# Merge stage: both norms applied where products leave PSUM, unscaled split tiles feed the next product, and the per-layer input split in a buffer of its own

## The chip, the cores and the metric

The kernel runs on one core of one Trainium2 chip. The metric is the device time of one execution in microseconds (us), from the first instruction to the end. Kernels are compared by the median of several executions on the same chip. The profile shows one such execution, instruction by instruction.

## The reference

Two transformer-like blocks run over 512 tokens of 1024 features, in fp32. The change lies in the last part of the second block:

```python
        merged = gates[..., 0, :] * (attn @ w_up_attn[i]) + gates[..., 1, :] * (rw @ w_up_rwkv[i])
        x = x + merged @ w_out[i]
        hf = rms_norm(x, norm_ffn[i])
        x = x + jnp.square(jax.nn.relu(hf @ w_ff1[i])) @ w_ff2[i]
        hp = rms_norm(x, norm_ple[i])
        x = x + (p[i] @ w_ple[i]) * jax.nn.sigmoid(hp @ w_ple_gate[i])
```

`rms_norm(x, g)` is `x * rsqrt(mean(x * x) + 1e-6) * g`, with the mean over the 1024 features of a token and the gain `g` per feature. The hidden width of the feed-forward part is 4096, and `p` has 256 features per token. The root is one number per token, and a product over features is linear, so it can be multiplied in before or behind a product; relu lets a positive factor through as well.

## The kernel before

Everything is held with features on the 128 partitions and the 512 tokens along the free dimension, so 1024 features are `KT` = 8 row tiles of 128 x 512. The merge stage (`merge_block`) takes the last quarter of the kernel's time.

**Products in three passes.** Each fp32 operand is split into a high part in TensorE's fp32r type and the low rest. One product step is three matmuls (`three_pass`): weights high by data high, weights low by data high, weights high by data low. A tile of output, 128 features by 512 tokens, takes 8 rows of 3 matmuls, so 24. The matmuls stand in lines 240 to 242, whichever phase they serve.

**The weight ring.** Weights come in slots of 128 x 2048, which hold two output tiles' columns. A ring of two raw buffers is filled by SyncE's queue. ScalarE copies a slot to `w_hi` (line 215), VectorE subtracts to get `w_lo` (line 228), each one slot ahead of TensorE and each only after TensorE has finished the slot that used the buffer before. `hi_next` and `lo_next` are these two steps; they stand first in every slot's body on their engines.

**The phases**, in order: `up` (4 slots, 16 short tiles), `out` (4 slots), then four times `ff1[g]` and `ff2[g]` (4 slots each), `ple` (1 slot, 8 tiles of two rows), `pgate` (4 slots). Output tiles go round four PSUM banks. TensorE waits for the tile four before it to have left PSUM (`tile_free`), and at a phase's first tile for all of the phase before it. At a phase's first tile it also waits, row by row, for the data (`ready`).

**Who takes the tiles out.** In `out` and `ff2`, VectorE adds the tile to `x` (line 2798). In `ff1`, ScalarE does Relu out of PSUM (2750) and Square (2752) into the high part, VectorE squares again and subtracts for the low part (2832, 2835). In `ple`, VectorE copies (2848). In `pgate`, ScalarE does Sigmoid out of PSUM (2770), VectorE multiplies by the `ple` tile and adds to `x` (2858, 2860), and SyncE stores.

**The norms.** During `out` and the last `ff2`, ScalarE squares each finished tile of `x` (2699), and GpSimd adds the squares up (`add_squares`). Behind the last tile, TensorE multiplies the sum by a matrix of ones (2673), ScalarE takes the root of 128 x 512 (2714), VectorE its reciprocal (2779), and for each of 8 rows VectorE multiplies `x` by gain and reciprocal (2785), ScalarE copies the high part (2719) and VectorE subtracts the low part (2788). Only then is a row ready for the next product. `p` is split on ScalarE (2759) and VectorE (2842) behind the last `ff2`, into `y_hi` and `y_lo`, ahead of `ple`.

The helpers `sum_tokens` (line 318), `spread_tokens` (327) and `on_diagonal` (333) exist already and serve the earlier stages. `sum_tokens` multiplies the squares, as the stationary operand, by a column of ones, 128 tokens at a time: the sum comes out with one token per partition, 128 x 4. `on_diagonal` puts these 512 numbers on the diagonals of four 128 x 128 matrices. `spread_tokens` multiplies ones by these matrices, and so copies the numbers into a row on all partitions, 128 x 512.

Of the kernel before, what the change touches and what calls it, by code (L numbers as in the profile page):

```python
# [21 lines left out]
P = 128  # L22
D = 1024
# [238 lines left out]
def gemm_slot(pe, nc, R, ph, j, q, r, u_hi, u_lo, outs, rows=range(KT), cols=SLOT, ready=None):  # L262
# [5 lines left out]
    for m in range(ph.tiles):  # L268
# [2319 lines left out]
def merge_block(nc, io, C, PV, h, attn_t, rw_t, gate_pre):  # L2588

    with ExitStack() as ctx:  # L2590
# [15 lines left out]
        for _ in range(GROUPS):  # L2606
# [19 lines left out]
        squared, summed, std_done, rs_done, normed, u_hi_done, u_done = (  # L2626
            sem(n) for n in ("squared", "summed", "std_done", "rs_done", "normed", "u_hi_done", "u_done"))
# [3 lines left out]
        relu_hi, relu_sq, relu_done, p_loaded, p_hi, p_done, ple_read, ple_gated, x_done, stored = (  # L2631
            sem(n) for n in ("relu_hi", "relu_sq", "relu_done", "p_loaded", "p_hi", "p_done", "ple_read", "ple_gated", "x_done", "stored"))
# [28 lines left out]
        @block.gpsimd  # L2661
        def _(pool):
            for n in range(2):
                if n:
                    pool.wait_ge(summed, n)
                add_squares(pool, nc, sq, sq_sum, squared, sq_added, n, KT)

        @block.tensor
        def _(pe):
            def norm(n):  # L2670

                pe.wait_ge(sq_added, KT * n)
# [9 lines left out]
            norm(1)  # L2682
            for g in range(GROUPS):
                products(ff1[g], u_hi, u_lo, ready=(u_done, 0) if g == 0 else None)
                products(ff2[g], y_hi, y_lo, ready=(relu_done, KT * g))
            pe.wait_ge(p_done, 1)
            products(ple, y_hi, y_lo, range(2), D)
            norm(2)
            products(pgate, u_hi, u_lo, ready=(u_done, KT))

        @block.scalar
        def _(act):
            def squares(n, ph):

                def tile(t):
                    act.wait_ge(R.tile_free, ph.c0 + t + 1)
                    if t >= 2:
                        act.wait_ge(sq_added, KT * (n - 1) + t - 1)
# [77 lines left out]
        def _(dve):  # L2776
            def norm(n):
                dve.wait_ge(std_done, n)
                nc.vector.reciprocal(rs, std).then_inc(rs_done, 1)  # L2779
                dve.wait_ge(rs_done, n)  # L2780
                for k in range(KT + 1):
                    if k < KT:
                        if k >= 4:
                            dve.wait_ge(u_done, KT * (n - 1) + k - 3)
# [202 lines left out]
```

## Time and profile before

| | |
|---|---|
| median of 3 runs | 2008.22 us (2004.9 to 2009.2) |
| the profiled execution's own time | 2009.05 us |
| its span, first to last instruction | 2007.2 us |
| TensorE matmul busy | 1792.2 us, 89% |
| TensorE weight load busy | 1533.6 us, 76% |
| VectorE busy | 1017.4 us, 51% |
| ScalarE busy | 670.2 us, 33% |
| GpSimd busy | 88.5 us, 4% |
| mean granted TensorE clock | 0.945 of full speed |

Times in the profile count from the start of the span. PE is TensorE, DVE VectorE, ACT ScalarE, POOL GpSimd, SPq SyncE's DMA queue. A matmul's bar is longer than its share of the pace, since matmuls overlap; the pace is read from one start to the next. The arrow at the end of a row names what ended the idle time before it.

### The profile page before, as it was taken

What the parts mean: (1) busy time and instruction counts of PE and PEld (TensorE: products, weight loads), DVE (VectorE), ACT (ScalarE), POOL (GpSimd) and SP (SyncE); (2) the same over time, 40 slices, a digit from 0 to 9 for tenths busy, and PEclk for the clock granted to TensorE, in tenths of its full rate; (3) what the DMA queues carried; (4) which work ended last, traced back from release to release, by engine and by line L of the source; (5) the groups of instructions that cost most, each with busy time, mean ns of one, the idle gap of its engine ahead of it and who ended that gap; (6) DMA issues with size and microseconds to landing.
All of it is one profiled execution on the core that took longest, in us unless ns stands there. A gap on an engine that the chain in (4) does not pass through costs nothing. (4 is left out here: it accounts for less than half of the span.)

```text
span 2007.2 us, 38445 instructions
## 1 busy us (share of the span) xinstructions
PE 1792.2 (89%) x17084; PEld 1533.6 (76%) x17084; DVE 1017.4 (51%) x1505; ACT 670.2 (33%) x1091; POOL 88.5 (4%) x115
## 2 busy tenths in 40 slices
PE   5999789888999999988999948888679899999978
PEld 5898767888989989787677737767568688788867
DVE  4146564455644645456554346765655534343444
ACT  3242233433433423343332233333143323232322
POOL 6000000010000000100000000000002000000020
PEclk9999888988999999989999969999889899999999
DMA  5211130111222232312122100000052222222211
GB/s 156 85 64 43 54 105 1 59 49 52 96 101 89 84 105 85 105 59 84 64 79 93 39 23 4 4 4 10 2 220 85 71 97 95 94 98 91 102 66 63
DMA packets 29260, 144.57 MB, mean 72 GB/s; under 512 B 6315, under 2 KB 9659, under 8 KB 14508
## 3 DMA queue, kind: packets, MB, share of 16 engines
q1 hardware_dynamic: 25116, 134.10, 18.7%
q0 software_dynamic: 3696, 7.35, 1.2%
q8 instruction: 132, 2.16, 0.4%
q10 hardware_dynamic: 288, 0.73, 0.1%
q14 instruction: 28, 0.23, 0.0%
HBM read 134.82 MB, written 8.91 MB: 72 GB/s over the span
## 5 line engine op out<-in xcount | busy, mean ns | idle before, releaser
L228 DVE TENSOR_TENSOR w_w_lo<-w_w_raw,w_w_hi 128x2048 fp32r<-128x2048 f32 x67 | 153.5, 2291 | 182.3 <-ACT w_w_hi L215 181.9
L240 PE MATMUL f_bank<-u_hi,w_w_hi 128*128 128x258 f32 x704 | 203.3, 289 | 12.3 <-DVE w_w_lo L228 6.1
L241 PE MATMUL f_bank<-u_hi,w_w_lo 128*128 128x258 f32 x704 | 202.2, 287 | 0.0
L242 PE MATMUL f_bank<-u_lo,w_w_hi 128*128 128x258 f32 x704 | 200.7, 285 | 0.0
L240 PE MATMUL g_bank<-g_u_hi,g_w_hi 128*128 128x512 f32 x384 | 152.8, 398 | 17.1 <-DVE g_u_lo L2788 13.6
L241 PE MATMUL g_bank<-g_u_hi,g_w_lo 128*128 128x512 f32 x384 | 151.1, 394 | 0.0
L242 PE MATMUL g_bank<-g_u_lo,g_w_hi 128*128 128x512 f32 x384 | 151.1, 394 | 0.0
L240 PE MATMUL g_bank<-g_y_hi,g_w_hi 128*128 128x512 f32 x336 | 132.9, 396 | 18.5 <-DVE g_w_lo L228 11.7
L240 PEld LDWEIGHTS f_bank<-u_hi,w_w_hi 128*128 128x128 f32 x704 | 135.1, 192 | 13.7 <-issue 6.4
L215 ACT ACTIVATE g_w_hi<-g_w_raw 128x2048 fp32r<-128x2048 f32 x45 | 85.9, 1909 | 174.2 <-PE g_bank L242 171.8
L215 ACT ACTIVATE w_w_hi<-w_w_raw 128x2048 fp32r<-128x2048 f32 x67 | 127.6, 1904 | 32.0 <-PE f_bank L242 32.0
L242 PEld LDWEIGHTS f_bank<-u_lo,w_w_hi 128*128 128x128 f32 x704 | 136.0, 193 | 0.0
L241 PEld LDWEIGHTS f_bank<-u_hi,w_w_lo 128*128 128x128 f32 x704 | 135.3, 192 | 0.0
L242 PE MATMUL g_bank<-g_y_lo,g_w_hi 128*128 128x512 f32 x336 | 132.5, 394 | 0.0
L241 PE MATMUL g_bank<-g_y_hi,g_w_lo 128*128 128x512 f32 x336 | 132.3, 394 | 0.0
L228 DVE TENSOR_TENSOR g_w_lo<-g_w_raw,g_w_hi 128x2048 fp32r<-128x2048 f32 x45 | 103.2, 2292 | 48.3 <-ACT g_w_hi L215 48.1
L240 PEld LDWEIGHTS g_bank<-g_u_hi,g_w_hi 128*128 128x128 f32 x384 | 73.0, 190 | 40.0 <-issue 20.1
L1641 PE MATMUL a_bank<-u_hi,w_w_hi 128*128 128x512 f32 x240 | 99.4, 414 | 4.2 <-DVE a_shift L1878 3.6
L1643 PE MATMUL a_bank<-u_hi,w_w_lo 128*128 128x512 f32 x240 | 99.0, 412 | 0.0
L1645 PE MATMUL a_bank<-u_lo,w_w_hi 128*128 128x512 f32 x240 | 98.9, 412 | 0.0
L240 PEld LDWEIGHTS g_bank<-g_y_hi,g_w_hi 128*128 128x128 f32 x336 | 64.1, 191 | 34.5 <-issue 17.0
L2798 DVE TENSOR_TENSOR h<-g_bank,h 128x512 f32<-128x512 f32 x40 | 27.7, 692 | 115.0 <-PE g_bank L242 115.0
(460 smaller groups left out, 4047.5 us busy)
## 6 DMA issues: line engine op xcount, KB each, us to landing
g_w_raw<-in_w_ff SPq DMA_DIRECT2D x32, 1024.0 KB, 4.8
w_w_raw<-in_w_in SPq DMA_DIRECT2D x30, 1024.0 KB, 4.8
w_w_raw<-in_w_ffn_in SPq DMA_DIRECT2D x22, 1024.0 KB, 4.8
w_w_raw<-in_w_ffn_out SPq DMA_DIRECT2D x12, 1024.0 KB, 4.8
w_w_raw<-in_w_o SPq DMA_DIRECT2D x4, 1024.0 KB, 4.9
gate_pre<-rw_t POOLq DMA_DIRECT2D x16, 256.0 KB, 2.3
g_w_raw<-in_w_up SPq DMA_DIRECT2D x4, 1024.0 KB, 9.5
g_branch<-gate_pre SPq DMA_DIRECT2D x4, 1024.0 KB, 12.5
```

The source lines that it names most:

```text
L215: nc.scalar.activation(R.hi[:, r, 0:size], R.raw[:, r, 0:size], ACT.Copy).then_inc(R.hi_done, 1)
L228: nc.vector.tensor_tensor(R.lo[:, r, 0:size], R.raw[:, r, 0:size], R.hi[:, r, 0:size].bitcast(F32), ALU.subtract).then_inc(R.split, 1)
L240: nc.tensor.matmul(out, w_hi, u_hi, start=start, stop=False)
L241: nc.tensor.matmul(out, w_lo, u_hi, start=False, stop=False)
L242: return nc.tensor.matmul(out, w_hi, u_lo, start=False, stop=stop)
L1641: nc.tensor.matmul(tile_bank(g), w_hi, u_hi[:, k, :], start=k == 0, stop=False)
L1643: nc.tensor.matmul(tile_bank(g), w_lo, u_hi[:, k, :], start=False, stop=False)
L1645: last = nc.tensor.matmul(tile_bank(g), w_hi, u_lo[:, k, :], start=False, stop=k == KT - 1)
L2798: nc.vector.tensor_tensor(x[:, t, :], bank[:, (2 * r + m) % 4, :], x[:, t, :], ALU.add).then_inc(R.tile_free, 1)
```

## The change

Both norms are applied later. While `x` is finished tile by tile, ScalarE copies `x` times the gain to `y_hi` and VectorE makes `y_lo` from the same product, without the factor per token. `ff1` and `pgate` read these; the relu results go to `u_hi` and `u_lo` in exchange. The factor per token is applied to the tiles as they leave PSUM, both in `ff1` and in `pgate`, and both times on VectorE. In `ff1` VectorE takes over Relu with it, as one operation; in `pgate` VectorE multiplies, and ScalarE's Sigmoid then reads the result from SBUF.

The factor itself is computed with the small products: `sums` on TensorE behind the first tile of `ff1[0]` (or behind the fourth tile of `ple`), root and reciprocal on 128 x 4, `spread` behind the next tile of `ff1[0]` (or behind the first tile of `pgate`), and a copy from PSUM on ScalarE, for which VectorE waits. GpSimd adds seven squares instead of eight; the eighth is summed by TensorE directly. `p` is split right behind `up` into buffers of its own.

```diff
 def gemm_slot(...):
         last.then_inc(R.tile_done, 1)
+        if then:
+            then(m)
...
-        sq, std, rs = branch[:, 8:10, :], branch[:, 10, :], branch[:, 11, :]
+        p_hi, p_lo = sb("p_hi", [P, 2, GRID], F32R), sb("p_lo", [P, 2, GRID], F32R)
+        sq = branch[:, 8:10, :]
+        rows = sb("rows", [P, 3, GRID])
+        sq_sum, rs, diag = rows[:, 0, :], rows[:, 1, :], rows[:, 2, :].rearrange("p (a b) -> p a b", a=NB)
...
         @block.gpsimd
-                    pool.wait_ge(summed, n)
-                add_squares(pool, nc, sq, sq_sum, squared, sq_added, n, KT)
+                    pool.wait_ge(tok_sum, n)
+                add_squares(pool, nc, sq, sq_sum, squared, sq_added, n)
...
         @block.tensor
-            def norm(n):
-                pe.wait_ge(sq_added, KT * n)
-                nc.tensor.matmul(bank[:, 4, :], C("ones"), sq_sum, start=True, stop=True).then_inc(summed, 1)
+            def sums(n):
+                pe.wait_ge(sq_added, (KT - 1) * n)
+                sum_tokens(pe, nc, C, bank[:, 4, :], sq_sum, P, NB, True, False)
+                pe.wait_ge(squared, KT * n)
+                sum_tokens(pe, nc, C, bank[:, 4, :], sq[:, (KT - 1) % 2, :], P, NB, False, True).then_inc(tok_sum, 1)
+            def spread(n):
+                pe.wait_ge(tok_diag, n)
+                spread_tokens(pe, nc, C, [bank[:, 5, :]], diag, P, NB).then_inc(row_done, 1)
+            def after_first(j, m):
+                if j == 0:
+                    (sums, spread)[m](1)
+            def after_ple(j, m):
+                if m == 3:
+                    sums(2)
+            def after_gate(j, m):
+                if j == 0 and m == 0:
+                    spread(2)
-            norm(1)
             for g in range(GROUPS):
-                products(ff1[g], u_hi, u_lo, ready=(u_done, 0) if g == 0 else None)
-                products(ff2[g], y_hi, y_lo, ready=(relu_done, KT * g))
+                products(ff1[g], y_hi, y_lo, ready=(u_done, 0) if g == 0 else None, then=after_first if g == 0 else None)
+                products(ff2[g], u_hi, u_lo, ready=(relu_done, KT * g))
-            products(ple, y_hi, y_lo, range(2), D)
-            norm(2)
-            products(pgate, u_hi, u_lo, ready=(u_done, KT))
+            products(ple, p_hi, p_lo, range(2), D, then=after_ple)
+            products(pgate, y_hi, y_lo, ready=(u_done, KT), then=after_gate)
...
         @block.scalar
                     act.wait_ge(R.tile_free, ph.c0 + t + 1)
+                    nc.scalar.activation(y_hi[:, t, :], x[:, t, :], ACT.Copy, scale=gain(NORMS[n], t)).then_inc(u_hi_done, 1)
...
             def norm(n):
-                act.wait_ge(summed, n)
-                nc.scalar.activation(std, bank[:, 4, :], ACT.Sqrt, scale=1.0 / D, bias=EPS).then_inc(std_done, 1)
-            def norm_hi(n):
-                for k in range(KT):
-                    act.wait_ge(normed, KT * (n - 1) + k + 1)
-                    nc.scalar.activation(u_hi[:, k, :], tmp[:, k % 4, :], ACT.Copy).then_inc(u_hi_done, 1)
+                act.wait_ge(tok_sum, n)
+                nc.scalar.activation(stat, bank[:, 4, 0:NB], ACT.Sqrt, scale=1.0 / D, bias=EPS).then_inc(tok_std, 1)
+                act.wait_ge(row_done, n)
+                nc.scalar.activation(rs, bank[:, 5, :], ACT.Copy).then_inc(row_read, 1)
...
             each_slot(act, up, up_slot)
+            act.wait_ge(p_loaded, 16)
+            nc.scalar.activation(p_hi[:], p_raw[:], ACT.Copy).then_inc(p_hi_done, 1)
             squares(1, out)
-            norm(1)
-            norm_hi(1)
...
                 def relu_slot(j, q, r, g=g):
                     hi_next(act, nc, R, ff1[g], j, q, r)
+                    if g == 0 and j == 0:
+                        norm(1)
                     for m in range(2):
                         t = 2 * j + m
-                        act.wait_ge(R.tile_done, ff1[g].c0 + t + 1)
-                        if KT * g + t >= 4:
-                            act.wait_ge(relu_done, KT * g + t - 3)
-                        nc.scalar.activation(branch[:, 4 + t % 4, :], bank[:, (2 * r + m) % 4, :], ACT.Relu).then_inc(R.tile_free, 1)
                         act.wait_ge(R.tile_free, ff1[g].c0 + t + 1)
-                        nc.scalar.activation(y_hi[:, t, :], branch[:, 4 + t % 4, :], ACT.Square).then_inc(relu_hi, 1)
+                        nc.scalar.activation(u_hi[:, t, :], branch[:, 4 + t % 4, :], ACT.Square).then_inc(relu_hi, 1)
...
             weights(ple)
             norm(2)
-            norm_hi(2)
             def pgate_slot(j, q, r):
                 hi_next(act, nc, R, pgate, j, q, r)
...
-                    act.wait_ge(R.tile_done, pgate.c0 + t + 1)
-                    nc.scalar.activation(branch[:, 8 + t, :], bank[:, (2 * r + m) % 4, :], ACT.Sigmoid).then_inc(R.tile_free, 1)
+                    act.wait_ge(R.tile_free, pgate.c0 + t + 1)
+                    nc.scalar.activation(branch[:, 8 + t, :], branch[:, 8 + t, :], ACT.Sigmoid).then_inc(gated, 1)
...
         @block.vector
             def norm(n):
...
+                dve.wait_ge(tok_std, n)
+                nc.vector.reciprocal(stat, stat).then_inc(tok_rs, 1)
+                dve.wait_ge(tok_rs, n)
+                on_diagonal(dve, nc, C, diag, stat, P, NB).then_inc(tok_diag, 1)
+            def add_to_x(ph, n=None):
+                def low(t):
+                    dve.wait_ge(u_hi_done, KT * (n - 1) + t + 1)
+                    nc.vector.scalar_tensor_tensor(y_lo[:, t, :], x[:, t, :], gain(NORMS[n], t), y_hi[:, t, :].bitcast(F32),
+                                                   ALU.mult, ALU.subtract).then_inc(u_done, 1)
...
                         nc.vector.tensor_tensor(x[:, t, :], bank[:, (2 * r + m) % 4, :], x[:, t, :], ALU.add).then_inc(R.tile_free, 1)
+                        if n and t:
+                            low(t - 1)
                 each_slot(dve, ph, slot)
+                if n:
+                    low(KT - 1)
...
             each_slot(dve, up, up_slot)
-            add_to_x(out)
-            norm(1)
+            dve.wait_ge(p_hi_done, 1)
+            nc.vector.tensor_tensor(p_lo[:], p_raw[:], p_hi[:].bitcast(F32), ALU.subtract).then_inc(p_done, 1)
+            add_to_x(out, 1)
...
                     lo_next(dve, nc, R, ff1[g], j, q, r)
+                    if g == 0 and j == 0:
+                        norm(1)
+                        dve.wait_ge(row_read, 1)
                     for m in range(2):
...
+                        dve.wait_ge(R.tile_done, ff1[g].c0 + t + 1)
+                        if KT * g + t >= 4:
+                            dve.wait_ge(relu_hi, KT * g + t - 3)
+                        nc.vector.scalar_tensor_tensor(a, bank[:, (2 * r + m) % 4, :], 0.0, rs, ALU.max, ALU.mult).then_inc(R.tile_free, 1)
...
-                add_to_x(ff2[g])
-            dve.wait_ge(p_hi, 1)
-            nc.vector.tensor_tensor(y_lo[:, 0:2, :], p_raw[:], y_hi[:, 0:2, :].bitcast(F32), ALU.subtract).then_inc(p_done, 1)
+                add_to_x(ff2[g], 2 if g == GROUPS - 1 else None)
...
             norm(2)
+            dve.wait_ge(row_read, 2)
             def pgate_slot(j, q, r):
                 lo_next(dve, nc, R, pgate, j, q, r)
...
-                    dve.wait_ge(R.tile_free, pgate.c0 + t + 1)
+                    dve.wait_ge(R.tile_done, pgate.c0 + t + 1)
+                    nc.vector.tensor_tensor(branch[:, 8 + t, :], bank[:, (2 * r + m) % 4, :], rs, ALU.mult).then_inc(R.tile_free, 1)
+                    dve.wait_ge(gated, t + 1)
```

## Rows read from the trace of the kernel before

**Rows 1.** Groups by line and shape, 1440 to 2007 us: busy, mean ns, idle before.

```profile
L228 DVE TENSOR_TENSOR g_w_lo<-g_w_raw,g_w_hi 128x2048 fp32r<-128x2048 f32 x45 | 103.2, 2292 | 48.3 <-ACT g_w_hi L215 48.1
L215 ACT ACTIVATE g_w_hi<-g_w_raw 128x2048 fp32r<-128x2048 f32 x45 | 85.9, 1909 | 174.2 <-PE g_bank L242 171.8 <-DMA g_w_raw<-in_w_up 1.7 <-DVE g_u_lo L2788 0.8
...
L2798 DVE TENSOR_TENSOR h<-g_bank,h 128x512 f32<-128x512 f32 x40 | 27.7, 692 | 115.0 <-PE g_bank L242 115.0
...
L2752 ACT ACTIVATE g_y_hi<-g_branch 128x512 fp32r<-128x512 f32 x32 | 20.3, 633 | 1.0
...
L2785 DVE SCALAR_TENSOR_TENSOR g_branch<-h,params,g_branch 128x512 f32<-128x512 f32 x16 | 11.8, 747 | 0.1
```

**Rows 2.** Windows: PE, PEld, DVE, ACT, POOL busy (count); granted clock; DMA share; GB/s.

```profile
1562.00:1580.00 18.00, 9.56 (x22) 5.61 (x23) 13.41 (x17) 7.69 (x12) 1.26 (x1) 0.62 0.00 0
1709.00:1754.00 45.00, 43.80 (x192) 35.96 (x192) 16.09 (x14) 9.20 (x7) 0.00 (x0) 1.00 0.26 94
1936.00:1939.00 3.00, 3.00 (x9) 2.30 (x8) 2.65 (x2) 0.00 (x0) 0.00 (x0) 0.50 0.02 8
```

**Rows 3.** Timeline around the first norm: start, length, engine, line, instruction.

```profile
1561.02 0.69 DVE L2798 TENSOR_TENSOR h<-g_bank,h 128x512 f32<-128x512 f32 x1 [4.75 <-PE g_bank L242]
...
1579.60 0.50 PE L240 MATMUL g_bank<-g_u_hi,g_w_hi 128*128 128x512 f32 x1 [0.30 <-DVE g_u_lo L2788]
```

**Rows 4.** Timeline, last `ff2` tile to `pgate`.

```profile
1931.57 0.69 DVE L2798 TENSOR_TENSOR h<-g_bank,h 128x512 f32<-128x512 f32 x1 [4.75 <-PE g_bank L242]
...
1935.41 0.50 PE L240 MATMUL g_bank<-g_y_hi,g_w_hi 128*128 128x512 f32 x1 [3.87 <-DVE g_y_lo L2842]
...
1947.83 0.39 PE L242 MATMUL g_bank<-g_y_lo,g_w_hi 128*128 128x512 f32 x1
...
1948.26 0.69 DVE L2848 COPY g_branch<-g_bank 128x512 f32<-128x512 f32 x1 [0.67 <-PE g_bank L242]
...
1962.92 0.50 PE L240 MATMUL g_bank<-g_u_hi,g_w_hi 128*128 128x512 f32 x1 [0.30 <-DVE g_u_lo L2788]
```

**Rows 5.** Timeline, two ordinary changes of phase.

```profile
1619.49 0.60 ACT L2750 ACTIVATE g_branch<-g_bank 128x512 f32<-128x512 f32 x1 [4.18 <-PE g_bank L242]
...
1620.18 0.47 PE L240 MATMUL g_bank<-g_y_hi,g_w_hi 128*128 128x512 f32 x1 [0.73 <-issue]
...
1663.60 0.39 PE L242 MATMUL g_bank<-g_y_lo,g_w_hi 128*128 128x512 f32 x1
1664.02 0.69 DVE L2798 TENSOR_TENSOR h<-g_bank,h 128x512 f32<-128x512 f32 x1 [4.75 <-PE g_bank L242]
...
1664.86 0.47 PE L240 MATMUL g_bank<-g_u_hi,g_w_hi 128*128 128x512 f32 x1 [0.88 <-DVE h L2798]
```

**Rows 6.** Timeline, `up` to `out`.

```profile
1516.93 0.47 PE L240 MATMUL g_bank<-g_u_hi,g_w_hi 128*128 128x512 f32 x1 [0.83 <-issue]
...
1521.74 2.29 DVE L228 TENSOR_TENSOR g_w_lo<-g_w_raw,g_w_hi 128x2048 fp32r<-128x2048 f32 x1
```

**Rows 7.** Timeline, the same small products in the layer's attention stage.

```profile
850.68 0.39 PE L242 MATMUL f_bank<-f_y_lo,w_w_hi 128*128 128x512 f32 x1
851.12 1.05 PE L318 MATMUL a_bank<-consts,f_a 128*128 128x1 f32 x8
...
857.45 2.08 PE L327 MATMUL a_bank<-a_s,consts 128*128 128x128 f32 x8 [3.89 <-DVE a_s L333]
...
897.85 1.05 PE L327 MATMUL a_bank<-a_s,consts 128*128 128x128 f32 x8
898.66 0.36 PE L1604 MATMUL a_bank<-w_w_hi,u_hi 128*128 128x256 f32 x1
```

**Rows 8.** Groups by line and shape, whole kernel.

```profile
L1234 DVE SCALAR_TENSOR_TENSOR m_at<-m_bank,m_work 128x400 f32<-128x400 f32 x16 | 9.2, 575 | 28.6 <-PE m_bank L773 14.6 <-PE m_bank L777 14.0
```

**Rows 9.** Timeline, end of the kernel.

```profile
2002.78 0.60 ACT L2770 ACTIVATE g_branch<-g_bank 128x512 f32<-128x512 f32 x1 [4.84 <-PE g_bank L242]
...
2004.86 0.33 SPq L2658 DMA_DIRECT2D out<-h  x1
```

More of the change, by code:

```diff
@@ L259, in lo_ahead, with gemm_slot @@
     lo_slot(dve, nc, R, q + 1, r)
-def gemm_slot(pe, nc, R, ph, j, q, r, u_hi, u_lo, outs, rows=range(KT), cols=SLOT, ready=None):
+def gemm_slot(pe, nc, R, ph, j, q, r, u_hi, u_lo, outs, rows=range(KT), cols=SLOT, ready=None, then=None):
     pe.wait_ge(R.split, 2 * q + r + 1)
@@ L308, in add_squares @@
         if k:
-            pool.wait_ge(added, KT * n + k)
+            pool.wait_ge(added, count * n + k)
             nc.gpsimd.tensor_tensor(total, total, sq[:, k % 2, :], ALU.add).then_inc(added, 1)
@@ L2615, in merge_block @@
         p_raw = sb("p_raw", [P, 2, GRID])
-        sq, std, rs = branch[:, 8:10, :], branch[:, 10, :], branch[:, 11, :]
-        sq_sum_t = sb("sq_sum", [P, GRID])
-        sq_sum = sq_sum_t[:]
-        tmp = branch[:, 12:16, :]
+        p_hi, p_lo = sb("p_hi", [P, 2, GRID], F32R), sb("p_lo", [P, 2, GRID], F32R)
+        sq = branch[:, 8:10, :]
+        rows = sb("rows", [P, 3, GRID])
+        sq_sum, rs, diag = rows[:, 0, :], rows[:, 1, :], rows[:, 2, :].rearrange("p (a b) -> p a b", a=NB)
+        stat_t = sb("stat", [P, NB])
+        stat = stat_t[:]
         bank = ctx.enter_context(nc.psum_tensor("g_bank", [P, 8, 512], F32))
@@ L2625, in merge_block @@
         sq_added = sem("sq_added")
-        squared, summed, std_done, rs_done, normed, u_hi_done, u_done = (
-            sem(n) for n in ("squared", "summed", "std_done", "rs_done", "normed", "u_hi_done", "u_done"))
+        squared, tok_sum, tok_std, tok_rs, tok_diag, row_done, row_read, u_hi_done, u_done = (
+            sem(n) for n in ("squared", "tok_sum", "tok_std", "tok_rs", "tok_diag", "row_done", "row_read", "u_hi_done", "u_done"))
         split_hi, split_lo, gate_open, both, m_hi, m_done = (
@@ L2630, in merge_block @@
         gate_loaded = [sem(f"gate_loaded{k}") for k in range(4)]
-        relu_hi, relu_sq, relu_done, p_loaded, p_hi, p_done, ple_read, ple_gated, x_done, stored = (
-            sem(n) for n in ("relu_hi", "relu_sq", "relu_done", "p_loaded", "p_hi", "p_done", "ple_read", "ple_gated", "x_done", "stored"))
+        relu_hi, relu_sq, relu_done, p_loaded, p_hi_done, p_done, gated, ple_gated, x_done, stored = (
+            sem(n) for n in ("relu_hi", "relu_sq", "relu_done", "p_loaded", "p_hi_done", "p_done", "gated", "ple_gated", "x_done", "stored"))
         branches = (attn_t, rw_t)
@@ L2664, in _, with products @@
                 if n:
-                    pool.wait_ge(summed, n)
-                add_squares(pool, nc, sq, sq_sum, squared, sq_added, n, KT)
+                    pool.wait_ge(tok_sum, n)
+                add_squares(pool, nc, sq, sq_sum, squared, sq_added, n)
         @block.tensor
         def _(pe):
-            def norm(n):
-                pe.wait_ge(sq_added, KT * n)
-                nc.tensor.matmul(bank[:, 4, :], C("ones"), sq_sum, start=True, stop=True).then_inc(summed, 1)
-            def products(ph, hi, lo, rows=range(KT), cols=SLOT, ready=None):
-                each_slot(pe, ph, lambda j, q, r: gemm_slot(pe, nc, R, ph, j, q, r, hi, lo, outs, rows, cols, ready))
+            def sums(n):
[6 more added lines that the diff above has]
+                spread_tokens(pe, nc, C, [bank[:, 5, :]], diag, P, NB).then_inc(row_done, 1)
+            def products(ph, hi, lo, rows=range(KT), cols=SLOT, ready=None, then=None):
+                each_slot(pe, ph, lambda j, q, r: gemm_slot(pe, nc, R, ph, j, q, r, hi, lo, outs, rows, cols, ready,
+                                                            then and (lambda m: then(j, m))))
+            def after_first(j, m):
[7 more added lines that the diff above has]
+                    spread(2)
             pe.wait_ge(split_lo, 2)
@@ L2696, in tile @@
                     act.wait_ge(R.tile_free, ph.c0 + t + 1)
+                    nc.scalar.activation(y_hi[:, t, :], x[:, t, :], ACT.Copy, scale=gain(NORMS[n], t)).then_inc(u_hi_done, 1)
                     if t >= 2:
[L2698 removed]
+                        act.wait_ge(sq_added, (KT - 1) * (n - 1) + t - 1)
                     nc.scalar.activation(sq[:, t % 2, :], x[:, t, :], ACT.Square).then_inc(squared, 1)
@@ L2777, in norm @@
             def norm(n):
[L2778 to L2784, printed above, removed]
-                        nc.vector.scalar_tensor_tensor(tmp[:, k % 4, :], x[:, k, :], gain(NORMS[n], k), rs, ALU.mult, ALU.mult).then_inc(normed, 1)
-                    if k:
-                        dve.wait_ge(u_hi_done, KT * (n - 1) + k)
-                        nc.vector.tensor_tensor(u_lo[:, k - 1, :], tmp[:, (k - 1) % 4, :], u_hi[:, k - 1, :].bitcast(F32),
-                                                ALU.subtract).then_inc(u_done, 1)
-            def add_to_x(ph):
+                dve.wait_ge(tok_std, n)
[7 more added lines that the diff above has]
+                                                   ALU.mult, ALU.subtract).then_inc(u_done, 1)
                 def slot(j, q, r):
@@ L2834, in relu_slot @@
                         dve.wait_ge(relu_hi, KT * g + t + 1)
-                        nc.vector.tensor_tensor(y_lo[:, t, :], branch[:, 12 + t % 4, :], y_hi[:, t, :].bitcast(F32),
+                        nc.vector.tensor_tensor(u_lo[:, t, :], branch[:, 12 + t % 4, :], u_hi[:, t, :].bitcast(F32),
                                                 ALU.subtract).then_inc(relu_done, 1)
```

3 lines of the change are left out of this document (removed).

## Prediction

> **What bounds the kernel now.** I read the groups of instructions of the merge stage first. The two engines that feed the weight ring are idle far more than busy: ScalarE's ring copy waited 171.8 us for TensorE's last product, and VectorE's subtraction for the ring took 2.29 us per slot of about 11 us [rows 1]. So TensorE sets the pace, and only a place where TensorE is held up can be won. The windows show where. In an ordinary stretch of 45 us TensorE is busy 43.8 us at granted clock 1.00, that is 2.4 GHz; from 1562 to 1580 us it is busy about half and the clock is at 0.62, and between 1936 and 1939 us it works without a pause at 0.50, that is 1.2 GHz [rows 2]. The timeline names the three holes: the norm between `out` and `ff1[0]` [rows 3], the split of `p` ahead of `ple`, and the norm between `ple` and `pgate` [rows 4]. Everything else in the stage is eight ordinary changes of phase, each a wait for the last tile to leave PSUM [rows 5].
>
> The pitch of one matmul at full clock: the first of `ff2[0]` starts at 1620.18, the last of its 192 at 1663.60, so 0.227 us each [rows 5]. A tile of 24 takes 5.45 us, a slot 10.9 us.
>
> **First norm.** VectorE's addition of the last `out` tile starts at 1561.02. TensorE then reaches row 7 of the first `ff1` tile (its last three matmuls) at 1579.60, since rows 0 to 6 are done piecemeal behind the norm [rows 3]. That is 18.6 us, and 0.1 more for the slow restart, 18.7. After the change this transition is like that from `ff2` to `ff1`: addition at 1664.02, first matmul at 1664.86, 0.84 later [rows 5]; row 7 follows 21 pitches and 0.1 of restart later, at 5.7. `low(6)` and `low(7)` are ready 1.5 and 2.3 us after the addition starts (0.69, and 0.75 each [rows 1]), before rows 6 and 7 are reached. Gain 13.0 us.
>
> **Split of p.** It moves to the end of `up`. Before, the addition at 1931.57 was followed by the first `ple` matmul at 1935.41 [rows 4], 3.84 us; after, by 0.84. Gain 3.0. The `ple` matmuls ran from 1935.41 to the start of the last at 1947.83, 12.4 us for 47 pitches, where 0.227 each make 10.7 [rows 2, 4]. With the hole gone I take the clock to stay up: gain 1.7. In its new place the split stands in the first `out` slot, ahead of the ring's copy on ScalarE and of its subtraction on VectorE. It has half the elements of those, so it costs at most 1.91 and 2.29 us [rows 1]. The subtraction, at 1521.74 before, then begins by 1524.1 and ends by 1526.4; TensorE asks for that slot at 1516.93 plus 10.9, 1527.8 [rows 6]. Covered with 1.4 us to spare even so; price nothing. Without that cover it would cost its excess alone, once.
>
> **Second norm.** From the last copy of `ple` at 1948.26 to row 7 at 1962.92 [rows 4], 14.7 and 0.1; after, 5.7 again. Gain 9.1. The gains add to 26.8 us.
>
> **What is put on TensorE.** `sums` is two calls of four products of one column, which the trace shows as two instructions each, sixteen in all; `spread` is eight. Eight of the former take 1.05 us including 0.25 of the last one's length, so 0.11 a piece, and the change of kind in front costs 0.2 (850.68 to 851.12, where 0.23 is usual) [rows 7]. Sixteen: 1.8, with 0.3 for both ends 2.1. For `spread`, 897.85 to 898.66 is 0.8, with the ends 1.1. Twice 3.2 is 6.4 us, all on TensorE's path. From below I take 0.1 each for 48, or 4.8; from above the row at half clock, 2.08 us for eight [rows 7], which makes `spread` and `sums` twice as dear, 12.8.
>
> **Evictions.** Relu moves from ScalarE (0.60) to VectorE, with the row of reciprocals multiplied in. Nearest rows: 0.75 for this operation with 512 columns from SBUF [rows 1], and 0.575 with 400 columns from PSUM [rows 8], so 0.69 to 0.75. At the end of `ff1` TensorE restarted 0.69 after Relu began [rows 5]; it would be about 0.9 after. Four times 0.2 is 0.8 us. The other tiles have free banks. VectorE's slot in `ff1` grows to 2.29 + 2 x (0.75 + 0.69 + 0.69), 6.6 of 10.9 us. The chain for the next slot is eviction 0.75, Square 0.63, ring copy 1.91, ring subtraction 2.29 [rows 1], with handoffs 5.9 after the last product, where 10.9 are there: 5 us to spare. Behind the wait stand the two relu steps and the next slot; neither is late.
>
> The Vector engine has a page in the Trainium skill, "VectorE: DVE Perf Modes", section "The TRN2 errata — SBUF-src ops pay a fixed extra latency per instruction", whose cycle table charges 120 fixed cycles for a PSUM source where an SBUF source pays 58, 62 more, or 0.065 us each. The rows show no such difference, 0.692 for the addition out of PSUM and 0.69 for those out of SBUF. By the page the moved evictions would cost about 0.3 us more over the five places where they end last, and the sum would be 1989.7.
>
> **The deferred row of reciprocals.** First norm, counted from the addition: `ff1` tile 0 ends at 6.4, `sums` at 8.5, the root, the reciprocal of four columns and the diagonal by 10.8 even if each took the 0.75 of a full row [rows 1], tile 1 at 13.9, `spread` at 15.0, its copy to SBUF at 15.8. The table load for the root lies before, while ScalarE waits. The first eviction is at 15.8, where TensorE needs the bank at 25.9. ScalarE's next ring copy waits for the second Square, near 19.4, then 1.9 and 2.3: slot 2 is split at 23.8, asked for at 25.9. 2 us to spare. In `ple`, `sums` fills TensorE while VectorE still works on the ring (until 6.2, then its first copy), so tile 4 doesn't wait. Second norm, from the last copy: tile 0 ends at 6.4, `spread` 7.5, the copy 8.2, and only then ScalarE's ring copy for slot 1 (10.1) and VectorE's subtraction (12.5). TensorE asks for it at 7.5 + 5.45, 13.0. Half a microsecond to spare: the tightest place of the change. Slot 2: two evictions, two sigmoids and four vector steps put its split at about 21.5, against 23.9.
>
> **Tail.** Before: sigmoid at 2002.78, store issued at 2004.86 [rows 9]. After, a multiplication of 0.69 comes in front with its handoff, 0.75 us more. The store behind it is unchanged.
>
> **Sum.** 26.8 - 6.4 - 0.8 - 0.75 is 18.85 us. The profiled execution took 2009.05 us by its own time (span 2007.2) and lies 0.8 above the median of 2008.22. Against the median: 2008.2 - 18.8 = 1989.4 us.
>
> **Rivals.** (a) The clock falls in or behind the small products, which use one column: `sums` and `spread` then cost up to twice as much and a dozen matmuls behind each run at 0.43 instead of 0.227. For both `sums` that is 2 x (2.1 + 1.7) = 7.6 us, 1997. For it: the fall to 0.50 after the hole at 1932. Against it: ordinary changes with 0.9 us idle leave it at 1.00 [rows 2, 5], and at 898 such products ran among others at full pitch [rows 7]. "TensorE: Matmul & The Clock Gate" in the Trainium skill, section "The HAM clock gate (the "warmup" mystery)", has the clock go down for want of activity; by that rule alone, removing the holes would leave it up throughout. The rows of the three holes agree. (b) Slot 1 of `pgate` comes late, as its ring copy now stands behind the row's copy: with 0.5 us to spare, a chain 2 us longer costs 1.5 us, 1991. (c) VectorE starves the ring in `ff1`. Sixteen slots: it ends slower than before only if each loses over 18.8 / 16 = 1.2 us, and 5 are spare first, so the chain must be 6.2 us longer than worked out, which needs evictions near 4 us instead of 0.75. At 1.5 us lost per slot the time is 2013. No row points to it. (d) The change does no net good: the norm's wait only moves to the first eviction. It needs the row 10 us later than worked out, in both norms; about 2008.
>
> **Chances.** Forecast 0.68, (a) in part or full 0.13, (b) 0.13, (c) 0.03, (d) 0.03. Range: low, with the inserts at their lower bound and ends of chains 1 us better, 1986.5; high, with the clock rival nearly whole, 1996. The three runs before lie from 2004.9 to 2009.2, so I keep about a microsecond of scatter in each end: 1986.0 to 1996.0. Differences under 0.2% (4 us) can't be told from none here. Faster 0.94, same 0.03, slower 0.03.
>
> **What would show it.** Between the last addition of `out` and row 7 of `ff1[0]` 5.7 us; the first `ple` matmul 0.84 after the last addition, at granted clock 1.00 from 1900 to the end; sixteen and eight small instructions of 2.1 and 1.1 us, twice; from Relu's successor to the next matmul 0.9; slot 1 of `pgate` without a wait for the ring. A clock of 0.50 behind `sums`, a wait for the ring's subtraction in `ff1` or in `pgate`, or a bank wait at tile 4 of `ff1[0]` would make it wrong.

## The result and the profile after

The changed kernel takes 1986.62 us, the median of 4 runs from 1982.3 to 1989.43; the one before 2008.2. The ratio is 0.9893, with a 95% interval of 0.9872 to 0.9915. The profiled execution has a span of 1985.2 us, 22.0 less. Timed again later, the ratio was 0.9893 once more (0.9870 to 0.9915).

Whole executions differ by several us before the merge stage begins: its first matmul started between 1464.8 and 1477.6 us in the fourteen profiles of this study. So I compare the **stage time**, from the first matmul of `up` to the end of the span. It is 537.5 us before and 515.4 after (515.6 in a second profile), 22.1 less. Of this, 0.2 lies in `up`, which the change doesn't touch: its matmuls take 45.9 us before and 45.7 after. In all fourteen profiles `up` takes 44.9 to 46.1, so a few tenths between two stage times can be scatter.

The windows of the changed kernel, columns as in [rows 2]:

```profile
1562.00:1580.00 18.00, 18.00 (x93) 15.28 (x92) 7.77 (x11) 6.33 (x9) 0.00 (x0) 1.00 0.16 59
1921.00:1936.00 15.00, 13.72 (x67) 11.39 (x68) 9.94 (x14) 3.23 (x4) 0.00 (x0) 1.00 0.20 70
1949.00:1981.00 32.00, 30.94 (x137) 25.30 (x135) 17.89 (x22) 7.71 (x9) 0.00 (x0) 1.00 0.21 81
```

The window from 1562 to 1580, about half empty and at a clock of 0.62 before [rows 2], is now full at 1.00. So is everything to the end of the stage, but for the changes of phase.

The timeline behind the last addition of `out`; L320 and L329 are the two kinds of small product, L2853 the new eviction:

```profile
1560.81 0.69 DVE L2808 TENSOR_TENSOR h<-g_bank,h 128x512 f32<-128x512 f32 x1 [2.51 <-PE g_bank L242]
...
1561.60 0.47 PE L240 MATMUL g_bank<-g_y_hi,g_w_hi 128*128 128x512 f32 x1 [0.83 <-issue]
...
1566.46 0.39 PE L240 MATMUL g_bank<-g_y_hi,g_w_hi 128*128 128x512 f32 x1
...
1567.14 0.95 PE L320 MATMUL g_bank<-consts,g_rows 128*128 128x1 f32 x8
...
1568.84 0.49 PE L240 MATMUL g_bank<-g_y_hi,g_w_hi 128*128 128x512 f32 x1
...
1574.43 1.05 PE L329 MATMUL g_bank<-g_rows,consts 128*128 128x128 f32 x8
1575.24 0.47 PE L240 MATMUL g_bank<-g_y_hi,g_w_hi 128*128 128x512 f32 x1
...
1576.15 0.69 DVE L2853 SCALAR_TENSOR_TENSOR g_branch<-g_bank,g_rows 128x512 f32<-128x512 f32 x1 [6.02 <-ACT g_rows L2739]
```

The transition that took 18.6 us [rows 3] is an ordinary one: 0.79 us to the first matmul, 5.65 to row 7. The small products take 1.7 and 0.8 us. The row of reciprocals is there in time; the first eviction starts at 1576.15, 10 us before its bank is wanted.

The same for the second half, to compare with [rows 4]:

```profile
1920.61 0.69 DVE L2808 TENSOR_TENSOR h<-g_bank,h 128x512 f32<-128x512 f32 x1 [2.50 <-PE g_bank L242]
...
1921.45 0.47 PE L240 MATMUL g_bank<-g_p_hi,g_w_hi 128*128 128x512 f32 x1 [0.88 <-DVE h L2808]
...
1934.46 0.69 DVE L2869 COPY g_branch<-g_bank 128x512 f32<-128x512 f32 x1 [0.67 <-PE g_bank L242]
...
1935.25 0.47 PE L240 MATMUL g_bank<-g_y_hi,g_w_hi 128*128 128x512 f32 x1 [0.83 <-issue]
...
1944.38 2.29 DVE L228 TENSOR_TENSOR g_w_lo<-g_w_raw,g_w_hi 128x2048 fp32r<-128x2048 f32 x1 [8.42 <-ACT g_w_hi L215]
...
1947.14 0.39 PE L240 MATMUL g_bank<-g_y_hi,g_w_hi 128*128 128x512 f32 x1
```

`ple` starts 0.84 us after the addition, `pgate` 0.79 after the last copy began. The last two rows are the tight place: the ring's subtraction ends at 1946.67, and slot 1 starts at 1947.14, on time. The 0.47 us between them less a handoff of 0.06 (1949.15 to 1949.21 in the late `spread` below) leaves 0.4 us to spare.

An end of `ff1` and the end of the kernel, to compare with [rows 5, 9]:

```profile
1608.19 0.69 DVE L2853 SCALAR_TENSOR_TENSOR g_branch<-g_bank,g_rows 128x512 f32<-128x512 f32 x1 [3.29 <-PE g_bank L242]
...
1608.98 0.47 PE L240 MATMUL g_bank<-g_u_hi,g_w_hi 128*128 128x512 f32 x1 [0.83 <-issue]
...
1979.98 0.69 DVE L2880 TENSOR_TENSOR g_branch<-g_bank,g_rows 128x512 f32<-128x512 f32 x1 [2.63 <-PE g_bank L242]
...
1982.81 0.33 SPq L2662 DMA_DIRECT2D out<-h  x1
```

From eviction to restart 0.79 us, where Relu had 0.69. The tail has grown from 2.08 to 2.83.

### The profile page after: what moved, and what is told of

Same layout as the page of the kernel before. It is cut to its first block and busy times, and to the rows that moved or that the text cites. A ratio compares the mean times of both kernels' runs of the same rounds, so it can differ in the third digit from the quotient of the medians.

```text
span 1985.2 us, 38515 instructions
## 1 busy us (share of the span) xinstructions
PE 1782.1 (90%) x17128; PEld 1530.5 (77%) x17128; DVE 1035.3 (52%) x1531; ACT 651.4 (33%) x1061; POOL 87.3 (4%) x113
## 5 line engine op out<-in xcount | busy, mean ns | idle before, releaser
L240 PE MATMUL g_bank<-g_y_hi,g_w_hi 128*128 128x512 f32 x384 | 151.2, 394 | 16.0 <-DVE g_w_lo L228 11.7
L241 PE MATMUL g_bank<-g_y_hi,g_w_lo 128*128 128x512 f32 x384 | 150.3, 392 | 0.0
L242 PE MATMUL g_bank<-g_y_lo,g_w_hi 128*128 128x512 f32 x384 | 150.2, 391 | 0.0
L228 DVE TENSOR_TENSOR g_w_lo<-g_w_raw,g_w_hi 128x2048 fp32r<-128x2048 f32 x45 | 108.4, 2408 | 48.3 <-ACT g_w_hi L215 48.2
L240 PE MATMUL g_bank<-g_u_hi,g_w_hi 128*128 128x512 f32 x320 | 125.1, 391 | 4.2 <-issue 4.2
L242 PE MATMUL g_bank<-g_u_lo,g_w_hi 128*128 128x512 f32 x320 | 124.5, 389 | 0.0
L241 PE MATMUL g_bank<-g_u_hi,g_w_lo 128*128 128x512 f32 x320 | 124.5, 389 | 0.0
L240 PEld LDWEIGHTS g_bank<-g_y_hi,g_w_hi 128*128 128x128 f32 x384 | 72.6, 189 | 33.7 <-issue 18.7
L242 PEld LDWEIGHTS g_bank<-g_y_lo,g_w_hi 128*128 128x128 f32 x384 | 72.7, 189 | 15.3
L241 PEld LDWEIGHTS g_bank<-g_y_hi,g_w_lo 128*128 128x128 f32 x384 | 72.7, 189 | 14.8
```

The costliest lines, as they stand in the source:

```text
L228: nc.vector.tensor_tensor(R.lo[:, r, 0:size], R.raw[:, r, 0:size], R.hi[:, r, 0:size].bitcast(F32), ALU.subtract).then_inc(R.split, 1)
L240: nc.tensor.matmul(out, w_hi, u_hi, start=start, stop=False)
L241: nc.tensor.matmul(out, w_lo, u_hi, start=False, stop=False)
L242: return nc.tensor.matmul(out, w_hi, u_lo, start=False, stop=stop)
```

## Experiments

Each is an edit of the kernel before or of the changed one. Where the table names no parent it is the changed kernel. Five of the kernels ran once: small products twice, apart; both with the second `spread` late; both with more VectorE operations. What is said of these rests on one profile each.

| kernel | stage time, us | against its parent |
|---|---|---|
| before | 537.5 | |
| p split early, alone (from before) | 532.6 | -4.9 |
| cheap root in place (from before) | 535.8 | -1.7 |
| after (from before) | 515.4 | -22.1 |
| p split late (from after) | 520.8 | +5.4 |
| small products twice in a row | 527.3 | +11.9 |
| small products twice, apart | 520.8 | +5.4 |
| second `spread` late | 522.0 | +6.6 |
| second `spread` late, ring first | 514.6 | -0.8 |
| one more VectorE operation a tile | 520.2 | +4.8 |
| two more | 562.2 | +46.8 |
| waits by bank | 505.9 | -9.5 |
| waits by bank, ring first | 504.6 | -10.8 |

**The split of p, one way and the other.** The same few lines moved in either kernel:

```diff
             each_slot(act, up, up_slot)
+            act.wait_ge(p_loaded, 16)
+            nc.scalar.activation(q_hi[:], p_raw[:], ACT.Copy).then_inc(p_hi, 1)
             squares(1, out)
...
             each_slot(dve, up, up_slot)
+            dve.wait_ge(p_hi, 1)
+            nc.vector.tensor_tensor(q_lo[:], p_raw[:], q_hi[:].bitcast(F32), ALU.subtract).then_inc(p_done, 1)
             add_to_x(out)
```

> The kernel before, with only the split of p moved behind up, into buffers of its own. Theory (the hole of 3 us ahead of ple costs itself and the half-clock stretch behind it): the first ple matmul follows the last addition by 0.84 us instead of 3.84, the ple matmuls take 10.7 us instead of 12.4, the granted clock stays at 1.00 from 1920 to 1945 us; span 2007.2 - 4.7 = 2002.5 us. Rival (the half clock comes from the phase itself, its short tiles of 6 matmuls, and not from the hole): only 3.0 us are gained, 2004.2, and a stretch at 0.50 stays. Rival (the split at its new place delays the first out slot): TensorE waits for the ring's subtraction near 1528 us, and up to 1.5 us of the gain are lost there.

Measured: ratio 0.9977 (0.9967 to 0.9987). In the kernel before with the early split:

```profile
1930.00 0.69 DVE L2799 TENSOR_TENSOR h<-g_bank,h 128x512 f32<-128x512 f32 x1 [4.75 <-PE g_bank L242]
...
1930.84 0.47 PE L240 MATMUL g_bank<-g_q_hi,g_w_hi 128*128 128x512 f32 x1 [0.88 <-DVE h L2799]
...
1934.00:1938.00 4.00, 4.00 (x20) 3.30 (x19) 3.96 (x6) 0.00 (x0) 0.00 (x0) 1.00 0.36 100
```

> The changed kernel, with the split of p put back behind the last ff2 (buffers of its own kept). Theory: the hole of 3 us comes back and with it the half clock, 3.0 + 1.7 us, span 1985.2 + 4.7 = 1989.9 us; the four columns sums stand in the slow stretch too, so up to 0.5 more. Rival (without a norm on the path, ple has its data earlier and the split hides): under 1 us. Rival (the clock falls only once in a while, by chance): 3.0 us, 1988.2, clock 1.00 behind the hole.

Measured: ratio to before 0.9929 (0.9913 to 0.9946), where the changed kernel has 0.9893. The profiled execution began its merge stage late, at 1477.6, so its span of 1998.4 says little. In the windows of the changed kernel with the late split:

```profile
1930.00:1934.00 4.00, 1.00 (x4) 0.85 (x5) 2.58 (x4) 3.49 (x4) 0.00 (x0) 0.97 0.00 0
1934.00:1937.00 3.00, 3.00 (x9) 2.35 (x8) 2.42 (x2) 0.00 (x0) 0.00 (x0) 0.50 0.09 22
```

The phases say it by themselves. With the early split in the kernel before, the stretch from `ff1[1]` to `ple` is 3.0 us shorter and `ple` 1.7; with the late split in the changed one, they are 3.4 and 1.65 longer. The clock of 0.50 behind the hole goes and comes with it: `ple` has such a stretch in all three profiles with the hole (before, cheap root, late split) and in one of the eleven without it, that of the small products twice in a row, of which more below. Both rivals, the phase itself or chance, fall. The third, that the split delays `out` at its new place, falls too: from its first matmul to its last `out` takes 43.67 us before, 43.66 with the early split alone and 43.67 after.

**Cheap root, norm in place.** The kernel before with `sum_tokens`, a root on 128 x 4, `on_diagonal` and `spread_tokens` in its `norm`, and the scaling ahead of the product as it was.

```diff
-                nc.tensor.matmul(bank[:, 4, :], C("ones"), sq_sum, start=True, stop=True).then_inc(summed, 1)
+                sum_tokens(pe, nc, C, bank[:, 4, :], sq_sum, P, NB, True, True).then_inc(summed, 1)
+                pe.wait_ge(tok_diag, n)
+                spread_tokens(pe, nc, C, [bank[:, 5, :]], diag, P, NB).then_inc(row_done, 1)
...
```

> The kernel before, with the sum, root and reciprocal of both norms on 128 x 4 and spread to a row by TensorE, but with the norm still applied ahead of the product as before. Theory (the gain of the change is that TensorE works while the factor is computed, and the cheap root is only what makes this small): per norm, 6.1 us from the sum to the reciprocal become about 4 to 5.5, the eight rows of scaling and splitting (9.8 us) stay; span 2007.2 - 3 = 2004 us, between 2002 and 2006. Rival (the reciprocal of 3.35 us over 128 x 512 and the long root were what cost the time, and the place hardly matters): over 10 us gained, below 1997.

Measured: ratio 0.9994 (0.9984 to 1.0004), no change that can be told; the stage 1.7 us shorter, where 3 were expected. Of these, 1.3 lie in the two norms (0.2 and 1.1, from the last addition or copy to row 7), the rest mostly in `up`. The timeline of its first norm:

```profile
1565.36 1.87 PE L318 MATMUL g_bank<-consts,g_sq_sum 128*128 128x1 f32 x8 [2.79 <-POOL g_sq_sum L310]
1567.27 0.17 ACT L2720 ACTIVATE g_stat<-g_bank 128x4 f32<-128x4 f32 x1 [2.00 <-PE g_bank L318]
...
1568.43 2.07 PE L327 MATMUL g_bank<-g_branch,consts 128*128 128x128 f32 x8 [1.20 <-DVE g_branch L333]
1570.54 0.60 ACT L2722 ACTIVATE g_branch<-g_bank 128x512 f32<-128x512 f32 x1 [3.10 <-PE g_bank L327]
```

The small products take 1.87 and 2.07 us here, twice what they take among full-size ones: the granted clock is 0.50 from 1565 to 1572. And there are two groups of them in the chain where there was one matmul pair of 2.00 us. So the cheap root alone is not the gain. The opposite, the long root deferred, was not run, and its rows in the kernel before make it a serious rival:

```profile
1563.77 2.00 PE L2673 MATMUL g_bank<-g_sq_sum,consts 128*128 128x512 f32 x2 [2.79 <-POOL g_sq_sum L310]
1565.80 0.60 ACT L2714 ACTIVATE g_branch<-g_bank 128x512 f32<-128x512 f32 x1 [2.13 <-PE g_bank L2673]
1566.43 3.35 DVE L2779 RECIPROCAL g_branch<-g_branch 128x512 f32<-128x512 f32 x1 [4.72 <-ACT g_branch L2714]
```

Its row is there 6.0 us after the sum begins; in the changed kernel it takes 9.0 (1567.14 to 1576.12). By estimate from these rows the long root would have been in time behind the first tile, with one pair of matmuls on TensorE instead of `sums` and `spread`. So deferring is what pays as far as is shown; that the cheap root was needed for it is not.

**Small products doubled.** A second issue of each, into banks that nothing reads.

```diff
+                sum_tokens(pe, nc, C, bank[:, 6, :], sq_sum, P, NB, True, False)
+                sum_tokens(pe, nc, C, bank[:, 6, :], sq[:, (KT - 1) % 2, :], P, NB, False, True)
...
+                spread_tokens(pe, nc, C, [bank[:, 7, :]], diag, P, NB)
```

> The changed kernel with all small products issued twice, the second time into banks 6 and 7, read by nothing. Theory (they cost their own pitch on TensorE and nothing else; in the trace 1.7 us for sums and 0.8 for spread): 2 x 2.5 = 5.0 us more, span 1990.2, clock still 1.00. In pgate slot 1 has 0.3 us of slack, which moves along with TensorE. Rival (the clock falls once the stretch of one-column products is 3.4 us long): a stretch at 0.50 behind them and 2 to 4 us more for each norm, 1994 to 1998. Rival (they are hidden behind waits of TensorE): under 2 us more.

Measured: ratio 0.9951 (0.9935 to 0.9968), the stage 11.9 us longer. Windows and timeline:

```profile
1567.00:1571.00 4.00, 4.00 (x34) 3.96 (x33) 0.00 (x0) 0.00 (x0) 0.00 (x0) 0.92 0.70 258
1571.00:1575.00 4.00, 4.00 (x10) 3.15 (x11) 0.87 (x2) 0.17 (x1) 0.00 (x0) 0.50 0.01 4
```

```profile
1567.23 1.84 PE L320 MATMUL g_bank<-consts,g_rows 128*128 128x1 f32 x16
1568.93 2.24 PE L320 MATMUL g_bank<-consts,g_branch 128*128 128x1 f32 x16
1571.03 0.77 PE L240 MATMUL g_bank<-g_y_hi,g_w_hi 128*128 128x512 f32 x1
```

Here the first rival was right and my theory of a linear price wrong. TensorE was busy without a pause, and yet the granted clock fell to 0.50 within the stretch of `sums`, which ran from 1567.2 to 1571.0. A mean of 0.92 from 1567 to 1571 puts the fall some 0.6 us before the end. It stayed at 0.50 for the full-size matmuls behind. `ple` shows the same.

> The same doubled small products as in the run that issued them twice in a row, but the second sums stands apart from the first: behind the third tile of ff1[0] and behind the seventh of ple. The work is the same, and no stretch of one-column products is longer than in the changed kernel. When they stood together, the granted clock fell to 0.50 inside the stretch and the merge stage took 11.9 us more than in the changed kernel (527.3 against 515.4, from its first matmul to the end). Theory (the unbroken length of such a stretch decides): clock 1.00 throughout, stage 515.4 + 2 x (1.7 + 0.8) + 0.2 for more restarts = 520.6. Rival (their number counts, or any such stretch may let the clock fall): a stretch at 0.50 again and 524 or more.

```diff
+                if j == 1 and m == 0:
+                    sums_again()
```

Measured: the stage at 520.8, as worked out, and the clock at 1.00 in every window:

```profile
1568.00:1572.00 4.00, 4.00 (x27) 3.60 (x26) 0.87 (x2) 0.17 (x1) 0.00 (x0) 1.00 0.79 262
1580.00:1584.00 4.00, 4.00 (x27) 3.57 (x25) 2.88 (x4) 2.44 (x2) 0.00 (x0) 1.00 0.00 0
1937.00:1941.00 4.00, 3.17 (x20) 2.53 (x20) 1.47 (x4) 0.00 (x0) 0.00 (x0) 1.00 0.00 0
```

The same number of products costs 5.4 us apart and 11.9 in a row. Only the place of the second `sums` differs, since `spread` is doubled in a row in both. So their number alone isn't what matters. The unbroken length explains it, but the second `sums` also stands further behind the pause of 1.2 us at the change of phase when it is moved; one long stretch far from a pause wasn't run.

**The tight place in `pgate`.**

```diff
-                if j == 0 and m == 0:
+                if j == 0 and m == 1:
                     spread(2)
```

> The changed kernel with the second spread behind the second tile of pgate instead of the first. The row's copy stands ahead of the ring's copy for slot 1 on ScalarE, and the wait for the row ahead of the ring's subtraction on VectorE. Theory (slot 1 of pgate has only about 0.3 us of slack, so the row's place sets it): the row comes one tile, 5.45 us, later, TensorE waits about 5.1 us for the subtraction; span 1985.2 + 5.1 = 1990.3. Rival (the tile four banks back or the sigmoid decides, the row has room): no wait for the ring, 1985.

Measured, one profile: TensorE waits 4.9 us for the ring's subtraction, and the matmul behind the wait runs at half clock:

```profile
1946.86 2.29 DVE L228 TENSOR_TENSOR g_w_lo<-g_w_raw,g_w_hi 128x2048 fp32r<-128x2048 f32 x1 [13.88 <-ACT g_w_hi L215]
...
1949.21 0.73 PE L240 MATMUL g_bank<-g_y_hi,g_w_hi 128*128 128x512 f32 x1 [4.88 <-DVE g_w_lo L228]
```

The stage is 6.6 us longer, 1.5 more than expected; that is the slow stretch, which I had left out although the same thing stood in my prediction for `p`.

> As with the late second spread, but in pgate ScalarE makes its ring copy and VectorE its ring subtraction for slot 1 ahead of the copy of the row and the wait for it. Theory (what hurt with the late spread is the ring behind the row, not the late evictions; four banks cover these): no wait for the ring in slot 1, span 1985 to 1986. Rival (the late row stalls the evictions, TensorE then waits for a bank or for slot 2): 1987 to 1991, with a bank wait or a ring wait at slot 2.

Measured: no wait, `pgate` 44.3 us as in the changed kernel. So the ring behind the row was what hurt. The 0.8 us less in the stage lie in `up`, which this edit doesn't touch.

**More work for VectorE in `ff1`.**

```diff
+                        for i in range(1):
+                            nc.vector.tensor_tensor(branch[:, 0:3, :], C.all[:, 0:GRID]..., C.all[:, GRID:2 * GRID]..., ALU.mult).then_inc(extra, 1)
...
```

> The changed kernel with one more VectorE operation of 128 x 1536 behind every relu tile, read from constants into space that nothing uses in ff1. That is 1.76 us a tile, 3.5 a slot, so VectorE has about 10.3 of 10.9 us of work in a slot. Theory (VectorE is off the path in ff1 with 4 to 5 us a slot to spare): within 1 us of 1985.2. Rival (the evictions moved to VectorE already sit near the edge): TensorE waits for the ring's subtraction in ff1, 5 to 20 us more.

Measured, one profile: 4.8 us more, of which 3.1 in `ff1[0]` and `ff2[0]` and 0.2 in the three groups behind. At the end of `ff1[0]`:

```profile
1607.16 1.75 DVE L2862 TENSOR_TENSOR g_branch<-consts 128x1536 f32<-128x1536 f32 x1
1608.95 0.69 DVE L2854 SCALAR_TENSOR_TENSOR g_branch<-g_bank,g_rows 128x512 f32<-128x512 f32 x1
...
1609.74 0.47 PE L240 MATMUL g_bank<-g_u_hi,g_w_hi 128*128 128x512 f32 x1 [2.28 <-issue]
```

VectorE starts late in `ff1[0]`, behind the row, and with 10.3 us of work in a slot of 10.9 it can't catch up there: the last eviction comes 1.5 us late, and behind the longer gap eight matmuls run at 0.43. The groups behind have no backlog and lose nothing. The store at the end took 1.2 us longer in this execution; I can't say why.

> The same extra operation twice per relu tile: 13.9 us of VectorE work against a slot of 10.9. Theory: here VectorE becomes the bound of ff1. A backlog of about 2.8 us a slot builds up, the last tile of ff1 leaves PSUM 8.5 us late for g = 1 to 3 and 15.5 late for g = 0, where VectorE starts 10 us later, and ff2 begins that much later: 41 us more, span 2026, at least 2015. Rival (the backlog is taken in by the ring and the banks): under 15 us more.

Measured: 46.8 us more, 16.6 in the first group (`ff1[0]` and `ff2[0]`) and about 10 in each later one; 41 were expected. VectorE can bind `ff1`, and does with about twice its work (13.9 us a slot instead of 6.6), not with 10.3: the prediction's rival (c) was far off.

**A version beating both.** The rest of TensorE's idle time were the changes of phase.

```diff
+        elif held:
+            pe.wait_ge(R.tile_free, ph.c0 + held[t])
         elif m == 0 and isinstance(j, int) and j == 0 and ph.c0:
             pe.wait_ge(R.tile_free, ph.c0)
...
+            HELD = {ph: (-3, -2, -1, 0) for ph in [out, *ff1, *ff2, ple]}
```

> The changed kernel, where a phase's first four tiles wait each for its own bank (the tile four before it has left PSUM) instead of all of the phase before; pgate, whose banks come in another order, keeps the old wait. Theory (what is left of TensorE's idle time in the stage are the changes of phase, 1.0 us of gap and 0.1 of restart each, and the data of the last tile are asked for only 5 us into the next phase): the gaps of ff1, ff2 and ple go, nine of them, 9 x 1.08 = 9.7 us; out gains nothing, its rows 4 to 7 come late anyway; span 1985.2 - 9.7 = 1975.5. Rival (the wait for the data takes the place of the wait for the bank: the last tile's eviction and split end too late for row 7): under half, 1980 or more, with TensorE waiting for VectorE's low part in the first tile of a phase.

> As with the waits by bank, and also pgate's first two tiles wait for their own banks (the seventh and eighth tile of ple), and in pgate the ring steps for slot 1 stand ahead of the row. Theory: one gap more is saved, about 0.7 of 1.1 us; the row's place is free of the ring; span 1974.8. Rival: slot 1 of pgate still waits for the ring by a few tenths, as everything on ScalarE and VectorE starts from ple's last tile: same time as with the waits by bank alone.

> The changed kernel itself, timed on the same chip as the two kernels with waits by bank, so that they can be compared with it. Expected 0.9893 of the kernel before, within 0.0022, span 1985.

Measured on one chip, against before: waits by bank 0.9838 (0.9815 to 0.9860), with the ring first 0.9832 (0.9808 to 0.9856), the changed kernel 0.9893. Medians 1976.7, 1975.9 and 1987.65 us. The timeline of the former, from `ff1[0]` to `ff2[0]`:

```profile
1604.84 0.39 PE L242 MATMUL g_bank<-g_y_lo,g_w_hi 128*128 128x512 f32 x1
...
1605.07 0.39 PE L240 MATMUL g_bank<-g_u_hi,g_w_hi 128*128 128x512 f32 x1
...
1605.27 0.69 DVE L2857 SCALAR_TENSOR_TENSOR g_branch<-g_bank,g_rows 128x512 f32<-128x512 f32 x1 [3.29 <-PE g_bank L242]
```

The first matmul of `ff2[0]` follows its predecessor by 0.23 us, before that predecessor's tile has left PSUM. The stage is 9.5 us shorter where 9.7 were expected. The nine gaps and restarts gave 10.0, from the last matmul of `out` to the last of `ple`; `out` gained nothing, as expected, and `up` was 0.4 longer in this profile. With `pgate` 1.2 more came, 1.0 of it in its gap. The two timed ratios alone can't tell these two versions apart; the phases can.

## Why the prediction was right

**1989.4 predicted, 1986.6 measured: 18.85 us of gain predicted, 22.0 in the profile.** Every step is where it was put, but several sizes were off, and all of them the same way. The result lies only 0.6 us above the low end of the range, so that it lies inside owes something to luck.

- *First norm, 13.0.* The step "TensorE then reaches row 7 at 1579.60" was a miscount. The rows of the kernel before:

```profile
1580.40 0.48 PE L240 MATMUL g_bank<-g_u_hi,g_w_hi 128*128 128x512 f32 x1
...
1580.73 0.39 PE L241 MATMUL g_bank<-g_u_hi,g_w_lo 128*128 128x512 f32 x1
...
1619.06 0.39 PE L242 MATMUL g_bank<-g_u_lo,g_w_hi 128*128 128x512 f32 x1
```

From 1580.73 to 1619.06, the start of the last matmul of `ff1[0]`, there are 38.33 us, 169 pitches of 0.2268. Had row 7 started at 1579.60, only 166 would be left at 1580.73. So TensorE was at row 6 there, and 1580.40, a slow restart, is row 7. A row is 0.7 us and its restart 0.1: the gain was 13.8, and likewise 9.9 instead of 9.1 for the second norm.
- *Split of p, 3.0 and 1.7.* Right in both parts, shown by the two moves (3.0 to 3.4, and 1.65 to 1.7).
- *Put on TensorE, 6.4.* It was 1.8 for `sums` and 0.9 for `spread`, with restarts, 5.5 in all. The 0.2 at the front, taken from a place where the stage changed too, didn't occur: from 1566.91, the start of the last full-size matmul, to 1567.14 is the usual pitch.
- *Evictions, 0.8.* The operation out of PSUM takes 0.69, not 0.75, and restarts came 0.79 after it began, not about 0.9: 0.1 each, 0.4. The Trainium skill's cycle table ("VectorE: DVE Perf Modes", section "The TRN2 errata — SBUF-src ops pay a fixed extra latency per instruction"), with 0.065 us more for PSUM, has no support here: in the changed kernel the 32 evictions of `ff1` take 0.691 us on average, the 32 multiplications from SBUF behind them 0.692.
- *Tail, 0.75.* 2.83 against 2.08: right.
- *Place of the row.* Both chains as worked out; 0.4 us of slack in `pgate` where 0.5 was given, shown by the late `spread`.

The corrected terms give 13.8 + 4.7 + 9.9 - 5.5 - 0.4 - 0.75, 21.75. The stage without `up` is 21.8 us shorter. Rival (a) didn't happen with `sums` of 1.7 us; with 3.8 us it did, clock and slow matmuls behind as it says. (b), (c) and (d) didn't happen.

## What to carry to other kernels

Apply a norm's factor where products leave PSUM, and put its computation in pieces between full-size products; the cheap root alone brought 1.3 us in two norms, too little to tell in the whole time, and whether the deferred factor needs it wasn't tried. Before adding small products to a busy TensorE, keep each stretch short (1.7 us held the clock here, 3.8 didn't) and look at the granted clock behind it. Wait for the bank that a tile needs, not for the phase before: that brought another half of what the whole change had.

## What the hardware showed beyond that

The granted clock can fall while the profile shows TensorE busy without a pause: 4.00 of 4.00 us with one-column products in the doubled run, and yet 0.92, then 0.50. "TensorE: Matmul & The Clock Gate" in the Trainium skill (section "Part 4: PE-mode transpose") says of transposes that they don't count as busy in the same way; it doesn't name narrow products, but these rows look the same. Why the clock fell isn't shown beyond that.

From start to start of two matmuls, gaps of 2.7 (one more VectorE operation), 3.8 and 9.0 (two more), 4.3 (before, ahead of `ple`), 4.7 (p split late) and 5.2 us (`spread` late) were followed by a stretch at half speed, the ordinary ones of 1.1 to 1.5 us never.

GpSimd and VectorE slowed each other in the changed kernel's `out` and last `ff2`, two rows of it:

```profile
1542.23 4.64 POOL L312 TENSOR_TENSOR g_rows<-g_rows,g_branch 128x512 f32<-128x512 f32 x2 [6.93 <-ACT g_branch L2722]
...
1542.34 3.38 DVE L228 TENSOR_TENSOR g_w_lo<-g_w_raw,g_w_hi 128x2048 fp32r<-128x2048 f32 x1
```

The ring's subtraction took 3.4 us instead of 2.29, beside two additions of GpSimd of 4.6 us together, where 1.3 is usual for one. It was hidden here. In the kernel before, the additions beside the ring's subtraction took up to 2.9 us, and the subtraction stayed at 2.29. "SBUF — State Buffer" in the Trainium skill (section "Who interferes with whom") says that a VectorE instruction with two SBUF inputs contends with a GpSimd instruction that reads SBUF; the trace agrees.
